# Cached-key scores as three rounded products in a two-layer retention and attention step

## What is computed

```python
def layer_sample(x, pos, ck, cv, s_ret, s_conv, p, lam_init):
    ...
    k_all = jnp.concatenate([ck.reshape(B, past, N_DIFF_HEADS, 2, DIFF_HD), k_d], axis=1)
    v_all = jnp.concatenate([cv, v_d], axis=1)
    o_d = diff_attn_block(q_d, pos, k_all, v_all, kpos, lam)

def diff_attn_block(q, qpos, k, v, kpos, lam):
    s = jnp.einsum('bqhcd,bkhcd->bhcqk', q, k) * (DIFF_HD ** -0.5)
    p = jax.nn.softmax(jnp.where(visible, s, -jnp.inf), axis=-1)
    a = p[:, :, 0] - lam * p[:, :, 1]
    return jnp.einsum('bhqk,bkhe->bqhe', a, v)
```

## Time and profile before

| | |
|---|---|
| median of 3 executions | 2145.59 us (2145.48 to 2145.66) |
| the profiled execution's own time | 2145.78 us |
| its span, first to last instruction | 2144.0 us |
| TensorE busy | 2127.2 us, 99% |
| VectorE busy | 1207.8 us, 56% |
| ScalarE busy | 971.2 us, 45% |
| GpSimd busy | 870.0 us, 41% |
| TensorE in the chain that ended last | 93% |
| granted TensorE clock, mean | 1.000 |

### The profile page before, as it was taken

How to read it: one execution, slowest core, us unless ns; L and a number is a source line. 1 busy time by engine, 2 the same in 40 slices (tenths; PEclk the granted TensorE clock), 3 DMA queues, 4 the chain that set the end, 5 groups by cost and what they waited for, 6 DMA issues and landing times.

```text
span 2144.0 us, 43228 instructions
## 1 busy us (share of the span) xinstructions
PE 2127.2 (99%) x17584; PEld 2064.4 (96%) x17584; DVE 1207.8 (56%) x2115; ACT 971.2 (45%) x1874; POOL 870.0 (41%) x386
## 2 busy tenths in 40 slices
PE   7999999999999999999999999999999999999999
PEld 7999999999999999999999999999999999999999
DVE  6676666656355652365267576766663555613651
ACT  5655564455233452354246655544542344423441
POOL 4344423235334443433463354323353434344334
DMA  5323222222222222321323233222222222223223
GB/s 178 101 85 115 75 81 79 68 92 79 85 93 79 99 67 82 108 90 61 108 92 103 77 104 100 68 68 94 84 80 79 86 92 81 79 89 99 99 67 106
DMA packets 75254, 191.63 MB, mean 89 GB/s; under 512 B 7632, under 2 KB 28720, under 8 KB 75056
## 3 DMA queue, kind: packets, MB, share of 16 engines
q1 hardware_dynamic: 66560, 182.41, 25.7%
q10 hardware_dynamic: 8496, 6.45, 0.9%
HBM read 175.41 MB, written 13.42 MB: 88 GB/s over the span
## 4 chain that ended last, share of the span: by engine, by line
PE 93%; DVE 4%; ACT 1%; issue 0%; DMA 0%; POOL 0%; DVEq 0%; ACTq 0%
PE ps L653 14%; PE ps L651 13%; PE ps L652 13%; PE ps L700 6%; PE ps L701 6%; PE ps L702 6%; PE ps L1085 4%; PE ps L1084 4%; PE ps L1086 4%; PE ps L679 2%; PE ps L723 2%; PE ps L837 2%; PE ps L871 2%; PE ps L805 2%; PE ps L797 2%; PE ps L799 1%
## 5 line engine op out<-in xcount | busy, mean ns | idle before, releaser
L516 POOL TENSOR_TENSOR wlo<-raw,whi 128x1024 fp32r<-128x1024 f32 (+1 forms) x328 | 768.9, 2363 | 1050.5 <-ACT whi L1145 1050.5
L651 PE MATMUL ps<-hl,whi 128*128 128x272 f32 x2432 | 704.3, 290 | 0.0
L653 PE MATMUL ps<-hl,wlo 128*128 128x272 f32 x2432 | 702.1, 289 | 0.0
L652 PE MATMUL ps<-hl,whi 128*128 128x272 f32 x2432 | 699.8, 288 | 0.0
L651 PEld LDWEIGHTS ps<-hl,whi 128*128 128x128 f32 x2432 | 459.1, 189 | 0.1
L653 PEld LDWEIGHTS ps<-hl,wlo 128*128 128x128 f32 x2432 | 458.2, 188 | 0.0
L652 PEld LDWEIGHTS ps<-hl,whi 128*128 128x128 f32 x2432 | 457.9, 188 | 0.1
L1145 ACT ACTIVATE whi<-raw 128x1024 fp32r<-128x1024 f32 (+1 forms) x330 | 314.2, 997 | 205.0 <-PE ps L1086 180.2
L700 PE MATMUL ps<-whi,hl 128*128 128x256 f32 x1216 | 347.2, 286 | 0.2
L701 PE MATMUL ps<-wlo,hl 128*128 128x256 f32 x1216 | 343.5, 283 | 0.0
L702 PE MATMUL ps<-whi,hl 128*128 128x256 f32 x1216 | 343.1, 282 | 0.0
(11 more groups left out here) (244 smaller groups left out, 3245.9 us busy)
## 6 DMA issues: line engine op xcount, KB each, us to landing
raw<-in_w_units_dram SPq DMA_DIRECT2D x260, 512.0 KB, 4.7
raw<-in_w_down_units_dram SPq DMA_DIRECT2D x64, 352.0 KB, 3.4
kcT<-in_cache_k_dram SPq DMA_DIRECT2D x16, 256.0 KB, 3.0
out_new_k_prompt_dram<-rawk SPq DMA_DIRECT2D x8, 512.0 KB, 3.0
out_new_v_prompt_dram<-vd SPq DMA_DIRECT2D x8, 512.0 KB, 3.6
raw<-in_w_first_dram SPq DMA_DIRECT2D x6, 512.0 KB, 4.8
vc_n<-in_cache_v_dram SPq DMA_DIRECT2D x8, 256.0 KB, 5.1
vc_n<-in_cache_v_dram ACTq DMA_DIRECT2D x8, 256.0 KB, 2.8
```

The lines of the kernel that those rows point to most:

```text
L516: e.tensor_tensor(wlo[:, s, a:b], raw[:, s, a:b], whi[:, s, a:b].bitcast(F32), ALU.subtract).then_inc(*S.up("w_ready", ("lo", j, part)))
L651: e.matmul(out, wh, hi, start=(c == 0), stop=False)
L652: e.matmul(out, wh, lo, start=False, stop=False)
L653: ins = e.matmul(out, wl, hi, start=False, stop=(c == KC - 1))
```

## The change

The scores of the sample rows against the cached keys become three products of rounded parts, as elsewhere in the kernel. ScalarE writes the high parts, VectorE the low ones. The buffer for the cached keys' parts (`kcR`, high and low) holds one head at a time: the first head's parts are made early in the body, the second head's while the steps run. The scores against the 32 new keys stay float32. The score waits for VectorE's low parts in place of the DMA and ScalarE.

The new buffers, and TensorE's `scores(n)`:

```diff
+            qsR = sb("qsR", [P, 2, 2, P], F32R, s)
+            kcR = sb("kcR", [P, 2, PAST], F32R, s)
...
                             acquire(bank, act=1)
-                            e.wait_ge(*S.at(f"cache_k{hh}", "in"))
-                            e.wait_ge(*S.at("act_step", ("qs", 1, 1)))
-                            st = qs[:, hh, :]
-                            e.matmul(pv(bank, P, PAST), st, kcT[:, hh, :], start=True, stop=True)
-                            ins = e.matmul(pv(bank, P, DEC, PAST), st, kdS[:, hh, :], start=True, stop=True)
+                            e.wait_ge(*S.at("dve_step", ("kc_lo", hh)))
+                            e.wait_ge(*S.at("dve_step", ("qs_lo", hh)))
+                            for i, (q, k) in enumerate(((0, 0), (1, 0), (0, 1))):
+                                e.matmul(pv(bank, P, PAST), qsR[:, hh, q, :], kcR[:, k, :], start=(i == 0), stop=(i == 2))
+                            ins = e.matmul(pv(bank, P, DEC, PAST), qs[:, hh, :], kdS[:, hh, :], start=True, stop=True)
```

ScalarE, whose first copy follows the first value tile, the second the exponentials of step 4:

```diff
+                    def cached_keys_hi(hh):
+                        e.wait_ge(*S.at(f"cache_k{hh}", "in"))
+                        e.activation(kcR[:, 0, :], kcT[:, hh, :], ACT.Copy).then_inc(*S.up("act_step", key=("kc", hh)))
...
                                 e.activation(buf[:, m, :], pv(bank, P, UC), ACT.Copy, scale=rs1[:, m:m + 1]).then_inc(
                                     *S.up(f"act_free_{bank}", (name, m)))
+                                if m == 0:
+                                    cached_keys_hi(0)
...
                                         e.activation(qs[rows, hh, c * DEC:(c + 1) * DEC], ps[rows, bank + SEQ:bank + TOK], ACT.Copy,
                                                      scale=DIFF_HD ** -0.5).then_inc(*S.up("act_step", key=("qs", hh, c)))
+                                    e.wait_ge(*S.own())
+                                    e.activation(qsR[:, hh, 0, :], qs[:, hh, :], ACT.Copy).then_inc(*S.up("act_step", key=("qs_hi", hh)))
...
                         if n + 2 < 10:
                             exps(n + 2)
+                        if n == 2:
+                            cached_keys_hi(1)
```

VectorE:

```diff
                         low_part(qdT, "q", hh, DIFF_HD ** -0.5)
+                    def cached_keys_lo(hh):
+                        e.wait_ge(*S.at("act_step", ("kc", hh)))
+                        e.wait_ge(*S.own())
+                        e.scalar_tensor_tensor(out=kcR[:, 1, :], in0=kcT[:, hh, :], scalar=1.0, in1=kcR[:, 0, :].bitcast(F32),
+                                               op0=ALU.mult, op1=ALU.subtract).then_inc(*S.up("dve_step", key=("kc_lo", hh)))
+
+                    cached_keys_lo(0)
+                    for hh in range(2):
+                        e.wait_ge(*S.at("act_step", ("qs_hi", hh)))
+                        e.wait_ge(*S.own())
+                        e.scalar_tensor_tensor(out=qsR[:, hh, 1, :], in0=qs[:, hh, :], scalar=1.0, in1=qsR[:, hh, 0, :].bitcast(F32),
+                                               op0=ALU.mult, op1=ALU.subtract).then_inc(*S.up("dve_step", key=("qs_lo", hh)))
                     for hh in range(2):
                         e.wait_ge(*S.at("act_step", ("khi", hh)))
                         low_part(kdT, "k", hh, 1.0)
...
+                        if n == 4:
+                            cached_keys_lo(1)
```

## The result

| | before | after |
|---|---|---|
| median | 2145.53 us (2145.41 to 2145.66, 4 runs) | 2170.2 us (2169.51 to 2170.76, 4 runs) |
| the profiled execution's span | 2144.0 | 2168.2 |
| granted TensorE clock, mean | 1.000 | 0.998 |

The change makes the kernel slower by 24.7 us, a ratio of 1.0115 (95% interval 1.0103 to 1.0127). The prediction said 19.4 us slower, 2165.0, with a range up to 2170: the sign and the two places are right, the size is short by 5 us, and the median lies 0.2 us outside the range.

What follows compares the result with a forecast made beforehand. TensorE, busy 99% of the span, was taken to bound the kernel. Eight bodies of 1.82 + 0.75 - 0.15 us gave 19.4 us on 2145.6, so 2165.0 us, range 2156 to 2170.

Steps and rivals of the forecast that it cites:

- the two places: VectorE's subtractions delay TensorE before the first scores (1.82 us per body) and before step 5's transposes (0.75).
- The products: On TensorE, three rounded products of 0.22 us replace 0.85 of fp32 per sample score: 0.19 saved, 3.0 in all.
- ScalarE's copies under cover: ScalarE's four added copies per body make nothing late on TensorE; the second only shifts GpSimd's next weight half 0.6 us.
- The cached keys held by GpSimd, ending 0.55 behind it: In both places, VectorE's cached keys subtraction starts under GpSimd's weight subtraction and ends 0.55 us after it.
- The chain: GpSimd's next piece 2.86, the first sample query 2.4, the second free: Before the first scores: GpSimd's second operation takes 2.86 us, holds the first sample query subtraction; the second takes 0.35.
- TensorE starts 0.05 behind the low part: First scores start 0.05 us after VectorE ends the first head's keys' low part, at 134.69 instead of 132.87.
- Its scores and everything behind them wait: TensorE runs its program in order, so the first scores and all later work shift by 1.82 us per body.
- Second place, 0.75: The second head's held cached keys subtraction delays TensorE's step 5 weight load by 0.75 us per body.
- The second score's saving stays: Of the second head's score saving of 0.19 us, 0.15 stays per body; the first score's is swallowed at step 5.
- The rival of the clock: An idle stretch of 1.8 us halves TensorE's clock, costing some 2 us in each of 8 bodies: 2181; chance 0.05.
- Not held: Rival: VectorE's new operations get through beside GpSimd, giving 2145, or 2143 with both savings whole; chance 0.07.
- No overlap: Rival: each held VectorE operation ends its full length after GpSimd, 2.24 and 0.95 us at the places: 2170; chance 0.07.

Runs made afterwards that it cites:

- e5: The changed kernel without VectorE's four subtractions, sample scores being three products of the high parts alone (not a usable version): 2143.17 us, ratio 0.9989.
- e2: The changed kernel with the two sample query subtractions moved behind the keys' low parts: 2151.52 us, ratio 1.0029.
- e10: e9 with the first head's cached keys subtracted ahead of the queries' low parts: 2144.95 us, ratio 0.9997.
- e1: The changed kernel with the second head's cached keys subtraction moved behind step 5's probabilities: 2168.77 us, ratio 1.0111.
- e6: The changed kernel with ScalarE's and VectorE's added work kept, but sample scores computed in fp32 as before: 2171.27 us, ratio 1.0117.
- e7: The changed kernel with the sample queries' low parts made from PSUM in four 64x32 operations, plus e1's edit: 2148.9 us, ratio 1.0017.
- e9: The changed kernel with the edits of e2 and e1 together: 2145.21 us, ratio 0.9998.

## Why the prediction came out as it did

- **The products.** Forecast 0.19 a score, 0.22 for a product. Measured 0.16 and 0.23 to 0.24 (e5, and the row of L846). The value taken lay between half of an fp32 record (0.21) and twice a product of 256 (0.24), and the upper end was right. Worth 0.4 us of a possible gain of 3.0.
- **ScalarE's copies under cover.** Right: e5 has them all and no new wait.
- **The cached keys held by GpSimd, ending 0.55 behind it.** Right. Forecast 2.05 and 1.45 long, measured 2.09 and 1.38; the end lies 0.55 behind GpSimd's in the second place.
- **The chain: GpSimd's next piece 2.86, the first sample query 2.4, the second free.** Right: 2.85, 2.29, 0.29. From the end of the queries' low parts to that of the first key tile 5.82 was forecast; 209.75 - 203.96 = 5.79 was measured. e2 shows the cause by moving the sample queries out from under GpSimd's second piece, e10 by moving the cached keys ahead of the first.
- **TensorE starts 0.05 behind the low part.** Wrong: 0.26. The 0.05 came from a weight load of the transposes, and this holds there again (229.53 to 229.59). Ahead of the first scores TensorE's queue has two semaphore instructions to get through, those of the waits in `scores` (third body, at 209.79 and 209.90, then the weight load at 209.98). That is 0.21 a body more than forecast, of which 0.16 is left in the stretch, 1.3 us in all; the chain ahead of it ran 0.03 shorter.

```profile
L831 PEldq EVENT_SEMAPHORE  x1: 51/51/51, 209.8 to 209.8; - x1
L832 PEldq EVENT_SEMAPHORE  x1: 51/51/51, 209.9 to 209.9; - x1
```

- **"Its scores and everything behind them wait" by one amount.** Wrong, and the largest miss in the bodies: this is the step that failed first. The second bank's scores have a wait of their own, for the low part of the second key tile, which before was covered. 0.33 a body, 2.6 us in all.
- **Second place, 0.75.** Right: 1.08 less the second bank's 0.33 is 0.75. e1 took 0.87 out of a body, with the first score's saving that comes back.
- **The second score's saving stays.** Right in kind: e6 confirms that only one of two savings is left (0.15 of 0.32). The stretch behind step 5 became 0.22 shorter where 0.15 was forecast, 0.16 of it by the score.
- **The rival of the clock, chance 0.05.** It came beside the forecast, in 2 of 8 bodies at 1.2 to 1.4 us instead of 8 at 2. The prediction treated it as another case and put none of it into the sum, which is the second step that failed, 2.6 us; what spoke against it was that before has no such gap, which was no evidence about a kernel that has one. The Trainium skill (TensorE: Matmul & The Clock Gate, section "What's actually happening") has the throttled state as the default and activity as what lifts it, and lists idleness as what brings it back, which the prediction left out; the rows agree that a pause can bring it back, and show that the same pause of 2.2 us does so in 2 of 8 bodies of the change and 5 of 8 of e1.
- **The other rivals.** "Not held" falls by the durations. "No overlap" would have given 2170, close to the measured time, and is wrong all the same: the held operations end 0.55 behind GpSimd, not the 0.75 of that case and not the 0.69 that they take alone, so the time agrees by chance. On the rule of the Trainium skill (SBUF — State Buffer, "Who interferes with whom") that the first one has the shared ports for its whole length: e10 agrees with it for the side that starts first, in the two bodies where VectorE's 693 ns start ahead and GpSimd's piece takes 2.69; for the loser 0.14 of its length is overlapped (0.69 ending 0.55 behind, 0.29 ending 0.15 behind), where the prediction took 0.2 from a length of 0.75.

In numbers, from 19.4 to the 24.2 by which the span grew: +1.3 (restart), +2.6 (second bank), -0.6 (steps 5 to 9), +2.6 (clock), -1.1 (the forecast counted eight full periods).

## What to carry to other kernels

Before adding work to an idle-looking VectorE, lay GpSimd's operations beside it: in these runs an operation with both operands in SBUF that started under GpSimd's subtraction took until GpSimd's end, whatever its size, and a second one behind it was caught by GpSimd's next. Put it ahead of GpSimd's start, or behind the operations that the next wait needs; and look at every body, since in one of them a few hundredths of a microsecond can decide over two. When a wait moves, follow each buffer that the waiting engine takes, not only the first one.

## What the runs showed of the chip that was not expected

- After one and the same pause of 2.2 us the granted clock of TensorE fell to half in some bodies and not in others of the same execution, 2 of 8 in the change and 5 of 8 in e1, between 0.03 us ahead of the first scores and 0.8 behind; in e6 it was 2 of 8, once as late as 2.1 behind. What picks the bodies is not known. The times of these kernels spread with it: e1 by 2.8 us over 4 runs and e7 by 4.5 over 11, where the kernel before, whole in its clock, spread by 1.5 over 15 and 1.6 over 21 beside them. So an edit that leaves such a stall can gain 7 us in the bodies and 1.4 in the median.
- TensorE's weight load came 0.05 behind VectorE's end for step 5's transposes, 0.12 for the second bank's first scores and 0.23 for the first scores, in one body (0.23 to 0.26 over all eight). Between that end and the load its queue has none, one (L609) and two semaphore instructions (L831, L832), which goes with 0.06 and then 0.11 more. No run took one out, so this is read from the rows and not tested.
- A held operation of VectorE gives its delay back to GpSimd: 2.83 to 2.87 instead of 2.37 to 2.40 for the next piece, in all bodies of the change, e1, e2 and e9, and 4.76 against 5.22 for the pair in e10 and e9.
